# The first block's feed-forwards take x without the norm's scale, which is put on the gate tiles and on the down product as they leave PSUM; the first norm has one ones product

## What is computed

```python
def swiglu(x, w_gate, w_up, w_down):
    return (jax.nn.silu(x @ w_gate) * (x @ w_up)) @ w_down
...
    for l in range(DEPTH):
        h = h + 0.5 * swiglu(rmsnorm(h, norm_gains[l, 0]), ffn_w_gate[l, 0], ffn_w_up[l, 0], ffn_w_down[l, 0])
        h = h + mixer(rmsnorm(h, norm_gains[l, 1]), ...)
        h = h + 0.5 * swiglu(rmsnorm(h, norm_gains[l, 2]), ffn_w_gate[l, 1], ffn_w_up[l, 1], ffn_w_down[l, 1])
```

## Time and profile before

| | us |
|---|---|
| median of 3 runs (lowest, highest) | 1894.01 (1892.62, 1894.32) |
| profiled execution, its time | 1892.72 |
| its span from first to last instruction | 1891.4 |
| TensorE busy | 1863.0 (98%) |
| VectorE busy | 1348.1 (71%) |
| ScalarE busy | 1045.7 (55%) |
| granted TensorE clock, mean | 0.998 of full |

### The profile page before, as it was taken

The page is one execution under the profiler, slowest core; times in us unless marked ns, Lnnn a source line. Parts: engine busy times, 40 slices in busy tenths (PEclk is TensorE's granted clock), DMA queues, the critical chain, the costliest instruction groups (busy, mean ns, idle before and its releaser), DMA issues.

```text
span 1891.4 us, 36376 instructions
## 1 busy us (share of the span) xinstructions
PE 1863.0 (98%) x15225; PEld 1821.5 (96%) x15225; DVE 1348.1 (71%) x2298; ACT 1045.7 (55%) x1764; POOL 1.3 (0%) x8
## 2 busy tenths in 40 slices
PE   7999999999999999999999999999999999999998
PEld 6999998899999999999889999999999999999998
DVE  5777666577776777667658777698877558787744
ACT  6444575655444544456566544576566457656643
POOL 0000000000000000000000000000000000000000
PEclk9999999999999999999999999999999999999999
DMA  6777343346786577733334878445455554455553
GB/s 245 275 260 267 120 137 110 108 161 221 262 295 221 177 261 269 267 124 129 112 118 173 301 268 300 159 158 170 164 193 184 180 176 169 160 175 182 187 190 112
DMA packets 51810, 365.91 MB, mean 193 GB/s; under 512 B 6620, under 2 KB 8060, under 8 KB 9920
## 3 DMA queue, kind: packets, MB, share of 16 engines
q1 hardware_dynamic: 51648, 363.59, 54.5%
HBM read 362.52 MB, written 1.05 MB: 192 GB/s over the span
## 4 chain that ended last, share of the span: by engine, by line
PE 94%; DVE 3%; ACT 2%; issue 1%; DMA 0%; SPq 0%; DVEq 0%; ACTq 0%
PE bank L441 28%; PE bank L442 27%; PE bank L443 27%; PE bank L477 2%; PE bank L473 1%; PE bank L474 1%; DVE w_lo L1541 1%; PE bank L712 1%; PE bank L640 1%; ACT w_hi L1022 1%; DVE full L1583 1%; PE bank L697 0%; PE bank L742 0%; PE bank L646 0%; DVE xn_lo L1547 0%
## 5 line engine op out<-in xcount | busy, mean ns | idle before, releaser
L441 PE MATMUL bank<-xn_hi,w_hi 128*128 128x272 f32 (+2 forms) x2624 | 758.8, 289 | 1.0 <-DVE w_lo L1541 1.0
L443 PE MATMUL bank<-xn_lo,w_hi 128*128 128x272 f32 (+2 forms) x2624 | 746.0, 284 | 0.0
L442 PE MATMUL bank<-xn_hi,w_lo 128*128 128x272 f32 (+2 forms) x2624 | 746.0, 284 | 0.0
L441 PEld LDWEIGHTS bank<-xn_hi,w_hi 128*128 128x128 f32 x2624 | 494.1, 188 | 8.9 <-issue 5.9
L442 PEld LDWEIGHTS bank<-xn_hi,w_lo 128*128 128x128 f32 x2624 | 494.0, 188 | 1.1
L443 PEld LDWEIGHTS bank<-xn_lo,w_hi 128*128 128x128 f32 x2624 | 494.8, 189 | 0.0
L1541 DVE TENSOR_TENSOR w_lo<-raw_b,w_hi 128x1024 fp32r<-128x1024 f32 (+1 forms) x282 | 356.6, 1265 | 145.6 <-ACT w_hi L1022 145.1
L1541 DVE TENSOR_TENSOR w_lo<-raw_a,w_hi 128x1024 fp32r<-128x1024 f32 (+1 forms) x282 | 356.3, 1265 | 140.7 <-ACT w_hi L1022 139.7
L1022 ACT ACTIVATE w_hi<-raw_a 128x1024 fp32r<-128x1024 f32 (+1 forms) x282 | 307.0, 1090 | 260.5 <-PE bank L443 221.9
L1022 ACT ACTIVATE w_hi<-raw_b 128x1024 fp32r<-128x1024 f32 (+1 forms) x282 | 306.9, 1089 | 250.3 <-PE bank L443 225.7
L441 PE MATMUL bank<-h_hi,w_hi 128*128 128x272 f32 (+1 forms) x704 | 201.8, 287 | 0.0
(11 more groups left out here) (322 smaller groups left out, 2718.3 us busy)
## 6 DMA issues: line engine op xcount, KB each, us to landing
raw_a<-in_weights SPq DMA_DIRECT2D x123, 1024.0 KB, 4.8
raw_b<-in_weights SPq DMA_DIRECT2D x123, 1024.0 KB, 4.8
ada_raw<-in_ada_w SPq DMA_DIRECT2D x48, 1024.0 KB, 4.9
raw_a<-in_weights SPq DMA_DIRECT2D x16, 1408.0 KB, 5.9
raw_b<-in_weights SPq DMA_DIRECT2D x16, 1408.0 KB, 5.9
c_rows<-in_c_rows SPq DMA_DIRECT2D x3, 512.0 KB, 3.7
raw_a<-in_weights SPq DMA_DIRECT2D x2, 768.0 KB, 4.1
raw_b<-in_weights SPq DMA_DIRECT2D x2, 768.0 KB, 4.2
```

Source lines behind the costliest of these rows:

```text
L441: pe.matmul(o, wh, xh, start=start, stop=False)
L442: pe.matmul(o, wl, xh, start=False, stop=False)
L443: return pe.matmul(o, wh, xl, start=False, stop=stop)
```

## The change

In the four feed-forwards of the first block `normalised` is replaced by `norm_scale`, which only waits for rstd. All units of stage 1 take the unscaled tiles, so there is one set of them. VectorE multiplies every gate tile by rstd from its bank into `gate`, and ScalarE's silu works on `gate` instead of the bank. The up tile stays unscaled, so h lacks one factor rstd, which the down product gets: VectorE makes 0.5 * bank * rstd in `full`, waits for that, and adds it to x. The mixers keep `normalised`. At the program's start the eight ones products become one, with the squares summed by VectorE; it stands between units 2 and 3, and units 2 and 3 are split before the squares. In `norm_scale` unit 3 of a stage is split before the root instead of behind it.

```diff
@@ sync_program
         elif (l, f) != (0, 0):
 
-            sp.wait_ge(*k.at("scaled", ("ffn", l, f, KD - 1)))
-            sp.wait_ge(*k.at("x_hi", ("ffn", l, f, KD - 1)))
+            sp.wait_ge(*k.at("sum_mm", ("ffn", l, f)))
...
@@ leading_units
         def norm(kk):
-            if stage == ("ffn", 0, 0):
-                if kk == 2:
-                    pe.wait_ge(*k.at("ones_in", 0))
-                for q in range(kk - 2, kk - 1 if kk < KD - 1 else KD):
-                    if q >= 0:
-                        pe.wait_ge(*k.at("square_a", q))
-                        pe.matmul(bank[7][:, TA], c.ones, c.first_sq[q % 4], start=q == 0, stop=q == KD - 1).then_inc(
-                            *k.up("square_mm", q))
-                free[7] = [("rstd", stage)]
-            elif kk == (2 if stage[0] in ("ln1", "ff") else 1):
+            if stage != ("ffn", 0, 0) and kk == (2 if stage[0] in ("ln1", "ff") else 1):
                 norm_sum(7, cols, stage)
         tiles_as_ready(u, 0, to, c.xn_hi, c.xn_lo, ("g", *stage), norm)
-        if to != TX:
+        if stage[0] == "mix":
             tiles_as_ready(u + 2, 2, to, c.xn_hi, c.xn_lo, stage)
         else:
             for i in (2, 3):
-                tile(u + i, i, TX, c.xn_hi, c.xn_lo)
+                if i == 3 and stage == ("ffn", 0, 0):
+                    norm_sum(7, cols, stage)
+                tile(u + i, i, to, c.xn_hi, c.xn_lo)
...
@@ scalar_program, ffn
-        normalised(stage, cols, to, u + 2)
+        norm_scale(stage, u + 2)
         load_table(SILU_SET)
         for i in range(FG):
             for b in range(4):
                 j = b - 2
-                if b >= 2:
-                    act.wait_ge(k.sem["unit_done"], u + 1)
-                    g = c.gate[:, j, to]
-                    if i:
-                        act.wait_ge(*k.at("gated", (l, f, i - 1, j)))
-                        act.activation(g, bank[gate_up_bank(i, j)][:, to], ACT.Silu).then_inc(*k.up("gate_a", (l, f, i, j)))
-                    else:
-                        act.wait_ge(*k.at("tile_v", ("gate", l, f, j)))
-                        act.activation(g, g, ACT.Silu).then_inc(*k.up("gate_a", (l, f, i, j)))
                 split_hi(u + 4)
-                if b >= 2:
+                if b < 2:
+                    g = c.gate[:, b, to]
+                    act.wait_ge(*k.at("tile_v", ("gate", l, f, i, b)))
+                    act.activation(g, g, ACT.Silu).then_inc(*k.up("gate_a", (l, f, i, b)))
+                else:
                     act.wait_ge(*k.at("gated", (l, f, i, j)))
...
@@ vector_program, ffn
-        normalised(stage, cols, to, c.v1[:, V_GAIN + 16 * f:V_GAIN + 16 * f + 8], u + 2)
-        for j in range(2):
-
-            dve.wait_ge(k.sem["unit_done"], u + j + 1)
-            dve.tensor_tensor(c.gate[:, j, to], bank[j][:, to], c.rstd[:, cols], ALU.mult).then_inc(*k.up("tile_v", ("gate", l, f, j)))
+        norm_scale(stage, u + 2)
         for i in range(FG):
             for b in range(4):
                 j, key = b - 2, (l, f, i, b - 2)
-                if b >= 2:
+                if b < 2:
+
+                    dve.wait_ge(k.sem["unit_done"], u + 1)
+                    if i:
+                        dve.wait_ge(*k.at("gated", (l, f, i - 1, b)))
+                    dve.tensor_tensor(c.gate[:, b, to], bank[gate_up_bank(i, b)][:, to], c.rstd[:, cols], ALU.mult).then_inc(
+                        *k.up("tile_v", ("gate", l, f, i, b)))
+                else:
 
                     dve.wait_ge(*k.at("gate_a", key))
-                    dve.wait_ge(*k.at("x_lo", ("h", l, f, i - 1, j) if i else (*stage, 6 + j)))
+                    dve.wait_ge(k.sem["unit_done"], u + 1)
+                    if i:
+                        dve.wait_ge(*k.at("x_lo", ("h", l, f, i - 1, j)))
...
                     m, b = 2 * g + s - 2, 4 + s - 2
                     dve.wait_ge(k.sem["unit_done"], u + 1)
-                    dve.scalar_tensor_tensor(out=c.x[:, m, cols], in0=bank[b][:, to], scalar=0.5, in1=c.x[:, m, cols], op0=ALU.mult,
-                                             op1=ALU.add).then_inc(*k.up("tile_v", ("dn", l, f, m)))
+                    part = c.full[:, m % 2, to]
...
+                    dve.scalar_tensor_tensor(out=part, in0=bank[b][:, to], scalar=0.5, in1=c.rstd[:, cols], op0=ALU.mult,
+                                             op1=ALU.mult).then_inc(*k.up("tile_v", ("dn_scaled", l, f, m)))
+                    dve.wait_ge(*k.newest("tile_v"))
+                    dve.tensor_tensor(c.x[:, m, cols], c.x[:, m, cols], part, ALU.add).then_inc(*k.up("tile_v", ("dn", l, f, m)))
```

More of the change, by code:

```diff
@@ L200, in __init__ @@
         self.full, self.gate = sb("full", [P, 2, T]), sb("gate", [P, 2, T])
-        self.first_sq = [self.sq[:, :], self.sq2[:, :], self.gate[:, 0, :], self.gate[:, 1, :]]
         self.raw = [sb("raw_a", [P, RAW_W]), sb("raw_b", [P, RAW_W])]
@@ L388, in load_vectors1 @@
         if l:
-            sp.wait_ge(*k.at("scaled", ("ffn", l - 1, 1, KD - 1)))
+            sp.wait_ge(*k.at("x_lo", ("g", "ffn", l - 1, 1, KD - 1)))
             sp.dma_start(c.v1[:, :], arg["vec1"][l]).then_inc(*k.up("vec_in", (1, l), by=16))
@@ L480, in tiles_as_ready @@
             if lead is not None:
-                if kk < KD - 1:
+                if kk < KD - 1 and stage[1] == "mix":
                     m.then_inc(*k.up("lead_mm", (stage, kk)))
@@ L524, in norm_sum @@
         pe.wait_ge(*k.at("sums", (key if key != ("ln1", 0) else "fn", KD - 1)))
+        if key == ("ffn", 0, 0):
+            pe.wait_ge(*k.at("ones_in", 0))
         if key == ("ln1", 0):
@@ L539, in ffn @@
                     tile(u + b, at, to, c.xn_hi, c.xn_lo)
-                free[at] = [("gated", (l, f, i, b - 2)) if b >= 2 else ("gate_a", (l, f, i, b)) if i else ("tile_v", ("gate", l, f, b))]
+                free[at] = [("gated", (l, f, i, b - 2)) if b >= 2 else ("tile_v", ("gate", l, f, i, b))]
             u += 4
@@ L555, in ffn @@
                     if half:
-                        free[b] = [("tile_v", ("dn", l, f, 2 * g + j))]
+                        free[b] = [("tile_v", ("dn_scaled", l, f, 2 * g + j))]
                     u += 1
@@ L1048, in normalised @@
         split_hi(held)
-        if stage == ("ffn", 0, 0):
-            split_hi(held + 1)
-        if stage == ("ffn", 0, 0):
-            act.wait_ge(*k.at("square_mm", KD - 1))
-            inverse_root(c.rstd[:, TA], bank[7][:, TA], 1.0 / D, "rstd", stage)
-        else:
-            root_of_mean(7, cols, stage)
+        root_of_mean(7, cols, stage)
         split_hi(held + 1)
@@ L1074, in norm_scale @@
         else:
-            root_of_mean(7, TB, stage)
+            root_of_mean(7, LIVE[stage[1]] if stage[0] == "ffn" and stage[2] else TA if stage[0] == "ffn" else TB, stage)
     def two_norms(stage):
@@ L1093, in from_input @@
         gain = c.v1[:, V_GAIN:V_GAIN + 8]
-        def square(kk):
-            if kk > 3:
-                act.wait_ge(*k.at("square_mm", kk - 4))
-            act.activation(c.first_sq[kk % 4], c.x[:, kk, :], ACT.Square).then_inc(*k.up("square_a", kk))
+        stage = ("ffn", 0, 0)
         load_table(LN_EXP_SET)
@@ L1104, in from_input @@
                 act.wait_ge(*k.at(f"x_in_{kk // 2}", 0))
-            before_norm(("ffn", 0, 0), kk, gain, TA, TA)
+            before_norm(stage, kk, gain, TA, TA)
             if kk == 1:
@@ L1108, in from_input @@
                 split_hi(1)
-            if kk > 1:
-                square(kk - 2)
-        square(KD - 2)
-        square(KD - 1)
+        split_hi(2)
+        split_hi(3)
+        for kk in range(KD):
+            square(kk, TA, stage)
         act.wait_ge(*k.at("ones_in", 0))
@@ L1714, in ffn @@
                     dve.wait_ge(k.sem["unit_done"], u + 1)
-                    dve.scalar_tensor_tensor(out=c.x[:, m, cols], in0=bank[b][:, to], scalar=0.5, in1=c.x[:, m, cols], op0=ALU.mult,
-                                             op1=ALU.add).then_inc(*k.up("tile_v", ("dn", l, f, m)))
+                    part = c.full[:, m % 2, to]
+                    if g == 0:
+                        dve.wait_ge(*k.at("x_lo", ("h", l, f, FG - 1, m)))
+                    else:
+                        dve.wait_ge(*k.at("tile_v", ("dn", l, f, m - 2)))
+                    dve.scalar_tensor_tensor(out=part, in0=bank[b][:, to], scalar=0.5, in1=c.rstd[:, cols], op0=ALU.mult,
+                                             op1=ALU.mult).then_inc(*k.up("tile_v", ("dn_scaled", l, f, m)))
+                    dve.wait_ge(*k.newest("tile_v"))
+                    dve.tensor_tensor(c.x[:, m, cols], c.x[:, m, cols], part, ALU.add).then_inc(*k.up("tile_v", ("dn", l, f, m)))
                 if not (g == 3 and s == 3):
@@ L2140, in vector_program @@
             split_lo(1)
+    split_lo(2)
+    split_lo(3)
+    for kk in range(1, KD):
+        add_squares(kk, TA, ("ffn", 0, 0))
     for l in range(L):
```

3 lines of the change are left out of this document (1 added, 2 removed).

## The result

| | us |
|---|---|
| before, median of 6 runs | 1893.97 (1891.63 to 1894.32) |
| changed, median of 6 runs | 1885.61 (1883.83 to 1887.43) |
| ratio | 0.996, 95% interval 0.995 to 0.997 |
| changed, profiled execution and its span | 1884.92, 1883.6 |

The kernel became faster by 8.4 us in the medians and by 7.8 us in the two profiled spans (1891.4 to 1883.6). The forecast was 1886.3.

The account below looks back on a forecast made before the run. TensorE, computing for 98% of the span, was taken as the bound, so only its waits count. Start -6.35, later beginnings -3.3, stage ends +1.9 give -7.7 us: 1894.01 to 1886.3 us, own range 1884.5 to 1888.0, wider range 1884.0 to 1890.5.

Parts of the forecast that it names:

- start, unit 4's first matmul: Program start: unit 4 begins at 27.6 us instead of 33.95, a gain of 6.35 us.
- new pause: Program start: TensorE stands 1.9 us before unit 4, waiting for that unit's weights.
- beginnings of (0,1), (1,0), (1,1): Starts of the later feed-forwards: losses of 0.99, 0.98 and 1.30 us go, 3.3 us gained.
- a dependent step at a stage end: Ends of the four feed-forwards: x's second VectorE instruction adds 0.48 us each, 1.9 us lost.
- VectorE in a group of four units: Gate stage: VectorE's work rises from 8.80 to 9.7 us of 12 and stays hidden.
- The clock: Rival: TensorE's clock falls after the new pause at the start, 1.6 us lost, total 1887.9; chance 0.14.
- The rival of the start: Rival: raw_b's transfer or the squares 3 us slower, start gains 3.3 instead of 6.35, total 1889.4; chance 0.06.
- VectorE as the bound in the gate stages: Rival: VectorE's evictions and low halves run late in every group; at 12.3 us a group, 1899.5 total; chance 0.07.

Follow-up runs that it names:

- e1: The change made only at the program's start and in feed-forward (0,0), the other three as in the kernel before: 1887.58 us against that kernel's 1892.34.
- e2: The change made only in feed-forwards (0,1), (1,0) and (1,1), start and (0,0) as in the kernel before: 1890.89 us against that kernel's 1892.34.
- e4: Changed kernel with the weight halves of units 4 and 5 made ahead of the root: 1882.14 us against 1892.34 of the kernel before.
- e6: Changed kernel with rstd left out of the down product, one VectorE instruction into x: 1883.22 us against 1885.38 of the changed kernel.
- e8: The changed kernel run again, nothing altered: 1885.38 us against 1892.68 of the kernel before.
- e3: Kernel before with only the start's single ones product and reordered squares and splits, tiles still scaled in all feed-forwards: 1889.68 us against 1892.34.
- e5: Changed kernel with the norm's product one k tile later in every stage that begins in the first block: 1882.18 us against 1892.68 before.
- e7: Changed kernel with units 4 and 5 split before the root and later norm products, except in mixers: 1881.00 us against 1892.68 before.
- e10: Changed kernel with the tenth ada piece's transfer issued one block of weights earlier: 1884.82 us, ratio 0.9962 to the kernel before.

## Why the prediction was right

| term | predicted | measured |
|---|---|---|
| start, unit 4's first matmul | 6.35 (at 27.6) | 6.60 (at 27.35) |
| new pause | 1.9 | 1.9 |
| beginnings of (0,1), (1,0), (1,1) | 0.99, 0.98, 1.30 | 0.97, 0.97, 1.43 |
| a dependent step at a stage end | 0.48, four times | 0.47 to 0.48 |
| VectorE in a group of four units | 9.7 of 12 | 9.5 of 12 |
| sum up to the second block's product | 7.7 | 8.1 |
| second block, to its next product | nothing | -0.3 |
| whole span, profiled executions | 7.7 | 7.8 |

**The sum.** The mechanism is the one forecast, and e1, e2, e4 and e6 show its terms. That the whole meets the forecast within 0.1 us is in part luck of the execution. The terms alone come to 8.1, and the second block, on which the prediction has nothing, gives 0.3 back (1209.92 to 1360.09, against 1218.06 to 1367.97). In e8, the same kernel once more, the same sum is 7.0 and the span 7.3 us shorter than before.

**The start.** The steps held one by one: no wait at units 2 and 3, the sum ready before the product, the root 0.7 us behind it. The clock rose at 15.88 instead of the 16.46 that the prediction took over; half a microsecond at full instead of half the clock is worth about 0.25 us, by my estimate, which is the difference. e3 adds how the gain of the start divides, 4.0 and 2.4 us of the chain, which the prediction had not separated. e4 shows that what the pause waited for is what I had named.

**The later beginnings.** e2 shows them alone. The 1.30 of (1,1) was worked with a step of 0.1185 us, which is too long: the kernel before takes 0.1167 in that stage's later groups and the changed one 0.117 at the beginning, hence 1.43.

**The ends.** e6 shows the price and that it adds in full, since the product already waited. e5 shows more than that: removing the wait paid in the feed-forwards and at the second block, and not in the mixers, which still scale their tiles.

**The rivals.** The clock had 0.14 and deserved about a half: it fell in three of six traces with this pause. The argument against it, dense matmuls on both sides, did not hold. Its price of 1.6 us was nearly right (1.5); its effect on the forecast is small because in these traces the executions in which it falls are those whose clock had risen early. The rival of the start did not come: block 1's weights are split from 12.10 on, and the sum of squares ends at 19.2. VectorE as the bound in the gate stages did not come, with 2.5 us to spare in 12; but a neighbour of it, VectorE late in the down stage of (1,1), took 0 and 0.5 us in two executions of the changed kernel and 2.4 of e7 once. The prediction, which looked at (0,1) and (1,0) for such covers, has nothing on that place.

**What stays open.** The interval of (1,1) is 188.30 before but 189.59 and 189.71 in e1 and e3, which are the same there. The rows say where: some 1.1 us in TensorE's step of 0.1178 instead of 0.1167 us through the gate stage, the rest mostly in a wait for a bank in the down stage. Whether the step belongs to these programs or to the execution is open; so the gain of (1,1) is 0.2 to 0.95 us against the one trace of the kernel before (e10 and the changed kernel), and over a microsecond more against e1 and e3.

## What to carry to other kernels

Where one engine runs without a gap, price a change by the places where that engine waits, and follow the chain up to the next thing it will wait for; that gave each term here within 0.25 us. A stage should be read in more than one execution before a term is called exact: (1,1) differed by 0.6 us between two of the same kernel. Scaling a result as it leaves PSUM instead of the input took the chain of scaled tiles behind the norm out of TensorE's way, and cost a dependent step at the place where the next norm wants its sum. Before moving a product behind a wait, look whether the stage behind it waits for the same chain.

## What the runs showed of the hardware

After a pause of 1.9 us (2.03 from matmul to matmul) TensorE's clock was at 1.2 GHz for about 3.4 us in e1, e5 and e10, from about a microsecond after work had resumed; the same pause, in kernels with the same start, left it at 2.4 GHz in the other three traces. The Trainium skill, "TensorE: Matmul & The Clock Gate", section "Why this matters for your kernels", puts the limit of a harmless pause near 3 us. The traces here don't agree: the one of e10, with 2.03 us from one matmul's start to the next, was followed by the low clock.

```profile
24.54 0.29 PE L441 MATMUL bank<-xn_lo,w_hi 128*128 128x272 f32 x1
26.57 0.39 PE L439 MATMUL bank<-xn_hi,w_hi 128*128 128x272 f32 x1 [1.74 <-DVE w_lo L1519]
```

The four middle intervals of the table, some 200 us with some 1580 matmuls each, repeat within 0.06 us between kernels and chips. The exceptions seen are short delays in a down stage ((0,1) to (1,0) is 0.15 us longer in e8 than in the changed kernel, (1,1) 0.6) and the step of (1,1) in e1 and e3. So a term of 0.5 us in a kernel of 1890 can be read in single traces, if a second execution confirms the stage, where medians of five runs leave an interval of about 2 us on either side.
